# x loaded first and stored by column blocks; the first pair's preparation moved into the V projection

## What is computed

```
x = x + 0.5 * swiglu(rms_norm(x, g), w_in, w_out)      # first of four FFNs
h = rms_norm(x, mix_norm)
r, k, v = xr @ w_rkv[0], xk @ w_rkv[1], xv @ w_rkv[2]   # token-shift mixes of h
w = -softplus(-(w0 + tanh(xw @ w1) @ w2)) - 0.5;  decay = exp(-exp(w))
a = sigmoid(a0 + (xa @ a1) @ a2)
kk = k * k_k / norm(k * k_k per head)
k = k * (1 + (a - 1) * k_a)
S_t = S_{t-1} diag(decay_t) + (S_{t-1} (-kk_t)) (kk_t * a_t)^T + v_t k_t^T ;  y_t = S_t r_t
...
return x                                               # 512 x 1024, after the last FFN
```

## Time and profile before

| | us |
|---|---|
| median of three runs | 2645.71 |
| lowest and highest run | 2644.31, 2650.67 |
| the profiled execution, device time | 2643.01 |
| its span (first to last recorded event) | 2641.3 |
| PE busy | 2549.0 (97%) |
| POOL, ACT, DVE busy | 982.9, 958.0, 805.3 |

### The profile page before, as it was taken

The page is one execution under the profiler, slowest core; times in us unless marked ns, Lnnn a source line. Parts: engine busy times, 40 slices in busy tenths (PEclk is TensorE's granted clock), DMA queues, the critical chain, the costliest instruction groups (busy, mean ns, idle before and its releaser), DMA issues.

```text
span 2641.3 us, 47025 instructions
## 1 busy us (share of the span) xinstructions
PE 2549.0 (97%) x18914; PEld 2142.8 (81%) x18930; DVE 805.3 (30%) x1295; ACT 958.0 (36%) x1599; POOL 982.9 (37%) x470
## 2 busy tenths in 40 slices
PE   6999999988998999999999999999999899999999
PEld 5888886767777788888899998888889777888887
DVE  3222014444554232220323012221034366322201
ACT  3222223533554233331434233332144565333321
POOL 3444442431222344444433434444443200444442
PEclk9999998988987899999999999999999999999999
DMA  3333222210000223323233433332232232333321
GB/s 129 96 95 95 96 83 80 92 40 4 5 4 17 75 88 95 95 96 97 94 128 119 160 121 119 95 95 96 96 105 87 65 112 65 97 99 98 95 96 64
DMA packets 180816, 230.39 MB, mean 87 GB/s; under 512 B 16473, under 2 KB 119033, under 8 KB 180665
## 3 DMA queue, kind: packets, MB, share of 16 engines
q1 hardware_dynamic: 180664, 228.20, 27.2%
HBM read 213.47 MB, written 14.68 MB: 86 GB/s over the span
## 4 chain that ended last, share of the span: by engine, by line
PE 94%; ACT 2%; DVE 2%; issue 1%; POOL 0%; SPq 0%; DMA 0%; DVEq 0%; ACTq 0%; POOLq 0%
PE bank L332 21%; PE bank L334 20%; PE bank L333 20%; PE bank L339 6%; PE bank L340 6%; PE bank L341 6%; PE bank L1169 1%; PE bank L1988 1%; PE bank L1282 1%; PE bank L2001 1%; PE bank L1252 1%; PE bank L2024 1%; PE bank L1300 1%; PE bank L1728 1%; PE bank L1484 1%
## 5 line engine op out<-in xcount | busy, mean ns | idle before, releaser
L307 POOL TENSOR_TENSOR w_lo<-w_raw,w_hi 128x1024 fp32r<-128x1024 f32 x376 | 904.7, 2410 | 1390.6 <-ACT w_hi L302 1390.0
L302 ACT ACTIVATE w_hi<-w_raw 128x1024 fp32r<-128x1024 f32 x376 | 395.3, 1058 | 1050.5 <-PE bank L334 876.9
L332 PE MATMUL bank<-xg_hi,w_hi 128*128 128x512 f32 x1408 | 551.0, 391 | 10.1 <-POOL w_lo L307 6.8
L334 PE MATMUL bank<-xg_hi,w_lo 128*128 128x512 f32 x1408 | 549.9, 391 | 0.0
L333 PE MATMUL bank<-xg_lo,w_hi 128*128 128x512 f32 x1408 | 549.7, 390 | 0.0
L332 PEld LDWEIGHTS bank<-xg_hi,w_hi 128*128 128x128 f32 x1408 | 265.6, 189 | 66.6 <-POOL w_lo L307 6.8
L333 PEld LDWEIGHTS bank<-xg_lo,w_hi 128*128 128x128 f32 x1408 | 265.7, 189 | 55.4
L334 PEld LDWEIGHTS bank<-xg_hi,w_lo 128*128 128x128 f32 x1408 | 265.4, 189 | 55.3
L332 PE MATMUL bank<-hid_hi,w_hi 128*128 (+1 forms) x704 | 274.4, 390 | 0.0
L333 PE MATMUL bank<-hid_lo,w_hi 128*128 (+1 forms) x704 | 274.0, 389 | 0.0
L334 PE MATMUL bank<-hid_hi,w_lo 128*128 (+1 forms) x704 | 273.9, 389 | 0.0
(11 more groups left out here) (283 smaller groups left out, 3137.4 us busy)
## 6 DMA issues: line engine op xcount, KB each, us to landing
w_raw<-in_ffn_w_in SPq DMA_DIRECT2D x352, 256.0 KB, 3.0
w_raw<-in_ffn_w_out SPq DMA_DIRECT2D x176, 256.0 KB, 2.7
w_raw<-in_w_kv SPq DMA_DIRECT2D x96, 256.0 KB, 3.1
w_raw<-in_rwkv_w_rkv SPq DMA_DIRECT2D x48, 256.0 KB, 2.9
w_raw<-in_attn_w_q SPq DMA_DIRECT2D x48, 256.0 KB, 3.0
k_dram<-stage SPq DMA_DIRECT2D x6, 1024.0 KB, 4.8
v_dram<-stage SPq DMA_DIRECT2D x6, 1024.0 KB, 5.6
keys<-k_dram SPq DMA_DIRECT2D x24, 256.0 KB, 3.5
```

What stands on the lines that cost most here:

```text
L302: act.activation(w_hi[:, s, :], w_raw[:, s, :], ACT.Copy).then_inc(w_hi_ready, 1)
L307: pool.tensor_tensor(w_lo[:, s, :], w_raw[:, s, :], w_hi[:, s, :].bitcast(F32), ALU.subtract).then_inc(w_lo_ready, 1)
L332: pe.matmul(o, hi, x_hi, start=start, stop=False)
L334: return pe.matmul(o, lo, x_hi, start=False, stop=stop)
```

## The change

**Start and end.** `start_load` is now called out of the first FFN's load: x first, then chunk 0, then the parameters, then chunks 1 to 3. The parameter DMAs of one source that adjoin become one (three DMAs in place of twelve, 15 in place of 24). ACT splits chunk 0 ahead of the parameter copies and chunks 1 and 2 behind the second and the fourth x tile. At the end, x is turned tile by tile (128 columns of all rows), ACT copies tiles 0 to 6 and DVE tile 7, and three stores take columns 0 to 511, 512 to 767 and 768 to 1023, with lines of 2, 1 and 1 KB.

**First pair.** The eighteen steps in `EARLY` leave the list for pair 0 and are written into the V projection. PE leaves banks 0 and 1 out of V's first rows (`row(2, k, ...)`) until `zwza`, the norms and `kkp` have used them, and then makes them up. The memory of the time mix is laid out anew for it, with `ar[2 - q % 3]` for `ar[q % 3]`. The attention's merge weights, which are already made in two parts in the kernel before, are the same in both kernels.

```diff
+EARLY = ("zwza", "tw", "ta", "dec", "undec", "pscan", "uscan", "pend", "tk", "kkp", "kk", "kka", "kp", "ara", "arr",
+         "bkb", "bkk", "rk")
...
-            if 0 <= q < pairs:
+            if 0 < q < pairs or q == 0 and kind not in EARLY:
...
+                if u == 0 and i % 2 == 1 and i < 2 * LEAD - 2:
+                    split_hi(act, i // 2 + 1)
...
+            if c0 == 0:
+                start_load(sp, lambda js: group(0, 0, js=js))
...
-        def start_load(sp):
-            for i, (_, v) in enumerate(vectors):
-                sp.dma_start(par_rows[(i % ROWS_A) * KT:(i % ROWS_A + 1) * KT, i // ROWS_A, :],
+        def start_load(sp, load_chunks):
+            for b in range(TB):
+                sp.dma_start(x_rows[:, b, :], x_in[0, b * P:(b + 1) * P, :]).then_inc(x_landed[b], 16)
+            load_chunks(range(1))
+            for first, n, v in PAR_LOADS:
+                sp.dma_start(par_rows[first % P:first % P + n * KT, first // P, :],
-            for b in range(TB):
-                sp.dma_start(x_rows[:, b, :], x_in[0, b * P:(b + 1) * P, :]).then_inc(x_landed[b], 16)
+            load_chunks(range(1, G_CHUNKS))
...
+            split_hi(act, 0)
             act.wait_ge(par_turned, 2)
             act.activation(par[:, 0:P], bank[0][:, 0:P], ACT.Copy).then_inc(par_ready, 1)
             act.activation(par[:, P:P + rows_b], bank[1][:, 0:rows_b], ACT.Copy).then_inc(par_ready, 1)
-            for c in range(LEAD):
-                split_hi(act, c)
...
-                        norms_act(act)
+                        tw_act(act, 0, 0)
+                        ta_act(act, 0, 0)
                 mix_hi_act(act, t, c0)
                 if t >= LEAD:
                     split_hi(act, c0 + t)
+                if t == 2 * KT + LEAD:
+                    act.wait_ge(resets_ready, 4)
+                    dec_act(act, 0, 0)
+                    undec_act(act, 0, 0)
+                    norms_act(act)
+                    tk_act(act, 0, 0)
+                    pend_act(act, 0, 0)
                 if t == LEAD:
                     lora_act(act)
...
+                if n == 2 * KT + LEAD:
+                    for half in range(2):
+                        pscan_dve(dve, 0, half)
+                    dve.wait_ge(norm_summed, 1)
+                    for half in range(2):
+                        uscan_dve(dve, 0, half)
+                    norms_dve(dve)
+                    dve.wait_ge(projection_copied, 8 + 1)
+                    kk_dve(dve, 0, 0)
+                    kka_dve(dve, 0, 0)
+                    ara_dve(dve, 0, 0)
+                    arr_dve(dve, 0, 0)
...
+            def row(i, k, ms):
+
+                t = i * KT + k
+                s, slot = (c0 + t) % SLOTS, t % RING
+                pe.wait_ge(w_lo_ready, c0 + t + 1)
+                pe.wait_ge(mix_lo_ready, t + 1)
+                for m in ms:
+                    if k == 0 and i == 0:
+                        if m == 0:
+                            pe.wait_ge(lora_ready, 2)
+                        if m == 1:
+                            pe.wait_ge(lora_gate_added, 1)
+                    elif k == 0:
+                        pe.wait_ge(projection_copied, 8 * (i - 1) + m + 1)
+                    if i < 2:
+                        last = products(pe, bank[m][:, :], s, m * P, mix_hi[:, slot], mix_lo[:, slot], k == 0, k == KT - 1)
+                    else:
+                        last = products_turned(pe, bank[m][:, :], s, m % 2 * 512,
+                                               mix_hi[:, slot, m // 2 * P:m // 2 * P + P],
+                                               mix_lo[:, slot, m // 2 * P:m // 2 * P + P], k == 0, k == KT - 1)
+                    if k == KT - 1 and m < 7:
+                        last.then_inc(projected, 1)
+                return last
+
+            for i in range(2):
...
-                    if k == 0 and i == 2:
-                        pe.wait_ge(projection_copied, 8 + 1)
-                        norms_pe(pe)
...
+                    row(i, k, FIRST_BANKS if i == k == 0 else range(8)).then_inc(w_used, 1)
+            pe.wait_ge(lora_landed, 16 * 6)
+            pe.wait_ge(projection_copied, 8 + 2)
+            zwza_pe(pe, 0, 0)
+            row(2, 0, range(2, 8))
+            after_read(pe, 0, "zw")
+            norms_pe(pe)
+            after_read(pe, 0, "za")
+            row(2, 0, (1,))
+            row(2, 1, range(1, 8))
+            kkp_pe(pe, 0, 0)
+            row(2, 2, range(1, 8))
+            after_read(pe, 0, "kk")
+            for k in range(3):
+                row(2, k, (0,)).then_inc(w_used, 1)
+            for k in range(3, KT):
+                row(2, k, range(8)).then_inc(w_used, 1)
 
 
...
-            pool.wait_ge(w_used, ph["c0"] + 3 * KT)
+            pool.wait_ge(norm_summed, 1)
...
-            split_lo_run(pool, ph["c0"] + LEAD, 3 * KT - LEAD)
+            split_lo_run(pool, ph["c0"] + LEAD, 2 * KT)
             pool_select(pool, ph)
+            split_lo(pool, ph["c0"] + 2 * KT + LEAD)
+            pool.wait_ge(projection_copied, 8 + 1)
+            for step in (kp_pool, bkb_pool, bkk_pool, rk_pool):
+                step(pool, 0, 0)
+            split_lo_run(pool, ph["c0"] + 2 * KT + RING, KT - RING)
...
-            pe.wait_ge(lora_landed, 16 * 6)
+            values_copied(pe, 1)
...
+        STORES = ((0, 4), (4, 6), (6, 8))
+
         def end_pe(pe, ph):
-            for b in range(TB):
-                for m in range(KT):
-                    if b == 0:
-                        pe.wait_ge(x_new, KT * ph["x"] + m + 1)
-                    last = pe.transpose(bank[2 * b + m // 4][:, (m % 4) * P:(m % 4 + 1) * P],
-                                        x[:, m, b * P:(b + 1) * P], ident[:, :])
+            for m in range(KT):
+                pe.wait_ge(x_new, KT * ph["x"] + m + 1)
+                for b in range(TB):
+                    last = pe.transpose(bank[m][:, b * P:(b + 1) * P], x[:, m, b * P:(b + 1) * P], ident[:, :])
                 last.then_inc(y_turned, 1)
 
+        def turned_rows(m):
+            return x_rows[:, :, m * P:(m + 1) * P], bank[m][:, :].rearrange("p (b d) -> p b d", d=P)
+
         def end_act(act, ph):
-            for b in range(TB):
-                act.wait_ge(y_turned, b + 1)
-                act.activation(x_rows[:, b, 0:512], bank[2 * b][:, :], ACT.Copy).then_inc(y_ready, 1)
+            for m in range(KT - 1):
+                act.wait_ge(y_turned, m + 1)
+                act.activation(*turned_rows(m), ACT.Copy).then_inc(y_ready, 1)
 
         def end_dve(dve, ph):
-            for b in range(TB):
-                dve.wait_ge(y_turned, b + 1)
-                dve.tensor_copy(x_rows[:, b, 512:1024], bank[2 * b + 1][:, :]).then_inc(y_right_ready, 1)
+            dve.wait_ge(y_turned, KT)
+            dve.tensor_copy(*turned_rows(KT - 1)).then_inc(y_right_ready, 1)
 
         def end_store(sp, ph):
-            for b in range(TB):
-                sp.wait_ge(y_ready, b + 1)
-                sp.wait_ge(y_right_ready, b + 1)
-                sp.dma_start(out[0, b * P:(b + 1) * P, :], x_rows[:, b, :]).then_inc(y_stored, 16)
-            sp.wait_ge(y_stored, 16 * TB)
+            for m0, m1 in STORES:
+                sp.wait_ge(y_ready, min(m1, KT - 1))
+                if m1 == KT:
+                    sp.wait_ge(y_right_ready, 1)
+                cols = slice(m0 * P, m1 * P)
+                sp.dma_start(out[0].rearrange("(b p) n -> p b n", p=P)[:, :, cols], x_rows[:, :, cols]).then_inc(y_stored, 16)
+            sp.wait_ge(y_stored, 16 * len(STORES))
```

More of the change, by code:

```diff
@@ L136, in build @@
+            tensors(c, both=((13352 + KT * T,), F32))
             with ExitStack() as c3:
@@ L192, in build @@
         PAR_QK = len(vectors) * KT
+        PAR_LOADS = [(PAR["ffn00"], 4, a["ffn_norm"].rearrange("l s d -> (l s d)")),
+                     (PAR["mix0"], 2, a["mix_norm"].rearrange("l d -> (l d)")),
+                     (PAR["mu0"], 6, a["rwkv_mu"].rearrange("l j d -> (l j d)"))]
+        PAR_LOADS += [(PAR[name], 1, v) for name, v in vectors[12:]]
         PAR_EXT = PAR_QK + 2 * NG
@@ L698, in build @@
         RWKV_CONSTS = 6 + 6 + 1
-        FIRST_BANKS = ([2, 3, 4, 6, 7, 5, 0, 1], range(8), [1, 2, 3, 4, 5, 6, 7, 0])
+        FIRST_BANKS = (2, 3, 4, 6, 7, 5, 0, 1)
         DECAY = float(np.exp(-0.5))
@@ L1125, in ara_dve @@
             need(dve, "y", q - 3)
-            done(dve.scalar_tensor_tensor(ar[:, q % 3, :, 0, :], pcum[:, :, 0:CH], -2.0, chunks(kk[:, :]),
+            done(dve.scalar_tensor_tensor(ar[:, 2 - q % 3, :, 0, :], pcum[:, :, 0:CH], -2.0, chunks(kk[:, :]),
                                           ALU.mult, ALU.mult), "ar")
@@ L1131, in arr_dve @@
             need(dve, "y", q - 3)
-            done(dve.tensor_tensor(ar[:, q % 3, :, 1, :], pcum[:, :, 1:CH + 1], chunks(r_all[:, q]), ALU.mult), "ar")
+            done(dve.tensor_tensor(ar[:, 2 - q % 3, :, 1, :], pcum[:, :, 1:CH + 1], chunks(r_all[:, q]), ALU.mult), "ar")
```

(6 more changed lines are left out.)

76 lines of the change are left out of this document (23 added, 53 removed).

## The result

| | before | changed |
|---|---|---|
| median, us | 2648.19 | 2618.02 |
| lowest and highest run | 2644.31, 2653.68 | 2616.03, 2622.47 |
| profiled execution: device time | 2643.01 | 2616.03 |
| its span | 2641.3 | 2614.3 |

A forecast was written before the change was run, and what follows sets the result against it. PE, 94% of the span, was taken to bound the kernel, with gains only where it idles, runs slow or at the end. 12.9 + 1.2 + 11.1 - 1.3 = 23.9 us off the median gave 2621.8 us, range 2614 to 2630.

The forecast's parts named there:

- What bounds: Whole kernel: PE is 94% of the span, so gains come only where PE idles, runs slow or does not end it.
- Loads and splits: 12.9: Start: x issued 8.13 us earlier, ACT's splits moved 2.8, first `xg_lo` without POOL beside it 1.95; together 12.9 us less.
- Clock at the start: 1.2: First FFN: full clock held through a 2 us gap, 2.05 gained, less 0.8 waiting for the fourth `xg_lo`; net 1.2 us.
- V pays 2.3: V projection: `zwza` and `kkp` now lie on PE's path, so V ends 2.3 us later, at most 2.3 + 5.
- The two thin places: In V: 0.4 us to spare ahead of `kkp`, 2.8 us ahead of the fifth chunk's `w_lo`.
- First pair: 11.1: Behind V: pair 0's preparation is already done, so the first `inv_x` comes at 583.3, not 594.42; 11.1 us, V's cost included.
- The table load: Ahead of pair 1's `tw`: ACT's extra load of 1.28 us is hidden in 1.90 us of idle time.
- The end: -1.3: Kernel's end: first store 0.9 us later and 1 KB lines 0.4 us slower, a loss of 1.3 us, ends at 0.3 and 1.8.
- the 3.0 in the prediction's last paragraph: Sign at the end: first store issued 3.0 us behind PE's last FFN matmul, 2.3 before the change.
- The sum and the rest: Whole kernel: 12.9 + 1.2 + 11.1 - 1.3 = 23.9 us less, a median of 2621.8 us, given 62%.
- the clock helps more: Rival, 8%: from 575 to 875 us, twenty us less at the low clock give 5 to 6 us more; 2616.
- The other rivals: V held, 13%, 2627; only x's move counts at the start, 8%, 2628; pair 0's preparation gives nothing, 5%, 2633; slower, 2%.

The follow-up runs named there:

- later traces of before: The kernel before executed a second and a third time with no edit; spans 2640.5 and 2647.0 us, ratio of before to itself 1.0002.
- the kernel with the parameters early: Changed kernel with the parameters turned ahead of x tile 5, not behind tile 7, and x loaded to a place of its own; ratio 0.9901.
- the second traces: The kernel before and the changed kernel each executed again with no edit; spans 2640.5 and 2621.0 us.

## Why the prediction was right, point by point

- **What bounds.** PE's idle time and clock, and the end. That everything between shifts along is true where PE streams; the recurrence and the stretch behind it move by 4 to 8 us of themselves.
- **Loads and splits: 12.9.** Against the first trace 11.5, and I first took the 1.4 for slower transposes in the changed kernel. The later traces of before set it right: 29.56 and 29.66 less 16.8 is 12.8. The step held; the trace that it was laid against was 1.3 us fast at this place. The parameters were in time.
- **Clock at the start: 1.2.** Failed in its mechanism: "I take it as held" was wrong. The clock fell behind 2.13 us of idle time too, for 3.7 us (the window of 0.55 above) where it had been 4.4. Nor did PE wait for the fourth `xg_lo`, the 0.8 us that I took off: at the low clock it eats more slowly. From the first matmul to the first `rstd` the gain was 0.6 us in the first pair of traces and 1.2 with the second trace of before (30.16 for 28.94). That this is my 1.2 is luck, since both of its parts were wrong. By the first `rstd` the start gave 13.9 us against that trace, 12.1 against the first; I had 14.1. A further 1.2 us up to R is the two-level stretch of the LoRA products, which I did not reckon with; the kernel before shows both of its levels, so this part is not shown to be the change's. Where the clock really was held is in the kernel with the parameters early, and there PE did wait for the fourth `xg_lo`, 0.6 us (0.8 forecast).
- **V pays 2.3.** V's copies come 53.04 us behind R's, for 50.50: 2.5. The two thin places held. `kkp` had 0.7 us to spare (0.4 forecast). The fifth chunk's `w_lo` ends at 541.1; by its matmuls PE comes to it at 543.0 (`kkp` 530.4, then 7, 3 and 8 banks at 0.70), 1.9 to spare (2.8 forecast).
- **First pair: 11.1.** 11.06, in every trace. DVE's copies set the first mask, as said, and 3.4 us (3.5 forecast) lie between mask and `inv_x`, at the full clock.
- **The table load** is hidden. By the rule of the Trainium skill (ScalarE: Activation LUTs, "What ACT_TABLE_LOAD costs") 0.8 us would have stuck out; the load ends at 575.15, `tw` starts at 575.76, and what it waited for is PE. No drain shows.
- **The end: -1.3.** Mis-sized, 1.8, the end of its bound. The first store goes out 3.4 us behind the last FFN matmul, 1.1 later than before, where 0.9 was forecast (the 3.0 in the prediction's last paragraph counts from the transposes, not from that matmul: 3.2 would have been meant). From the first store to the end it takes 7.7 us for 6.9, 0.7 more where 0.4 was forecast: the 1 KB lines go at 345 GB/s, as the loads in the earlier trace rows, and the 2 KB lines, which I had at the full rate, fall from 387 to 351. The Trainium skill (DMA: Bandwidth & Descriptors, "Specifications") asks 512 B for the full rate; here 410 GB/s with lines of 4 KB against 345 with 1 KB say otherwise.
- **The sum and the rest.** By the marks the change is worth 11.8 + 11.06 - 1.8 = 21.1 us against the first trace of before and 24.5 against the other two, of which 1.2 are the two-level stretch: 23.3 without it. Forecast 23.9. The profiled executions differ by 27.0, since the two kernels' first traces differ by 5.9 us behind the first inversion, and the second traces do not repeat that. My rival "the clock helps more" asked for such a gain (2616, twenty us less at the low level) and would have seemed right by the first pair of traces. It is not shown, and not wholly out. From the first to the last `inv_x`, where it put the gain, the two first traces show none (222.3 and 222.4 us); but the second and third trace of before take 225.4 and 229.5 there, and the means of the five traces without the new pair and of the nine with it are 226.6 and 223.5. Behind the last `inv_x` 1.3 of these 3.1 us are lost again, and by the last `rstd` 0.3 are left. The two comparisons of whole runs (24 to 36 us, and 21 to 30) both take in the 24.5.
- **The other rivals** are out: V was not held, x's move alone leaves PE's first FFN matmul 4.7 us later than the whole start does, pair 0's preparation gave all of its 11.1 us, and nothing was slower.

## What to carry to other kernels

Read a change from stretches of fixed work between two marks, each side in two or more traces: here the best of them repeat to 0.2 us while the whole moves by 6 us and more between executions of one program, and one trace of before can itself be the odd one. Make the stretches add up to the span, and look at the ones that ought not to have changed too: a difference there is chance or a mistake, and must not be booked to the change. Work that only waits for data known early (a first pair, parameters, a table) belongs beside a phase that streams at one engine's pace, with the spare time of each wait counted out. Count a wait of PE with what the clock takes behind it, and start the stores of a last result beside the work that makes its rest.

## What the hardware showed that I had not expected

- A wait of 4.2 us in a stream at the full clock cost 7.3 us. Idle times of 2.1 and 4.2 us were followed by the low clock, those of 0.7 and 1.2 us at the start were not. The granted clock still read 1.00 in the idle time of 2.1 us itself, so it must be looked for behind the gap, not in it.
- The 29 transposes take 4.77 us in one trace and 5.5 to 6.3 in the ten others that have them in one piece, with the same rows. The granted clock reads 1.00 in the slow and in the quick ones. What decides is open.
- One program, executed again, spends 350.7 or 354.7 us in its recurrence, and the kernel before 353.9 or 357.6 on one and the same chip. The Trainium skill (TensorE: Matmul & The Clock Gate, "Part 1: The HAM clock gate") says that the number of slow matmuls at a kernel's start varies from run to run; here the time of a stretch in the middle of a kernel does so too.
